# Norm, pick tables and mask of a fused four-layer kernel in PSUM banks, and two MLA steps in another order

## The reference, cut to what matters

```python
# 1. gMLP: layer norm of v (256 x 2048) ahead of the spatial product
u, v, g = jnp.split(rms_norm(h) @ w_in, 3, axis=-1)
v = layer_norm(v, ln_g, ln_b)                       # over 2048, one scale and one bias row
sv = jnp.einsum('gts,bcsgd->bctgd', wsm, v) + bs    # 16 groups, causal 128 x 128
y = u * sv * silu(g)
# 2. windowed attention ("b"): 16 heads of 64, keys of this and the block before, a sink per head
scores = jnp.where(mask, q @ k.T * 64 ** -0.5, -jnp.inf)
m = jnp.maximum(max(scores), sink)
p = exp(scores - m);  denom = sum(p) + exp(sink - m)
# 3. product-key experts, twice: 8 heads, 2 x 128 sub-keys, top 16 of each half
s1, i1 = top_k(s[:, :, 0], 16);  s2, i2 = top_k(s[:, :, 1], 16)
cand = s1[..., :, None] + s2[..., None, :]          # 16 x 16 sums of each head
top_s, pos = top_k(cand, 16)                        # pos // 16 picks from i1, pos % 16 from i2
# 4. MLA: c_q, c_kv, k_rope = split(x @ w_in); q = rms_norm(c_q) @ w_uq; kv = rms_norm(c_kv) @ w_ukv
```

## Time and profile before

| | us |
|---|---|
| median of 3 runs | 2416.28 |
| lowest, highest | 2414.76, 2420.68 |
| the profiled execution: its own time | 2416.68 |
| its span in the trace | 2414.9 |
| PE busy in the span | 2298.3 (95%) |
| PEld, DVE, ACT, POOL busy | 2100.4, 1470.9, 1167.3, 1175.9 |
| granted PE clock, mean | 0.986 of full |

### The profile page before, as it was taken

The page is one execution under the profiler, slowest core; times in us unless marked ns, Lnnn a source line. Parts: engine busy times, 40 slices in busy tenths (PEclk is TensorE's granted clock), DMA queues, the critical chain, the costliest instruction groups (busy, mean ns, idle before and its releaser), DMA issues. The chain is left out here.

```text
span 2414.9 us, 44964 instructions
## 1 busy us (share of the span) xinstructions
PE 2298.3 (95%) x15008; PEld 2100.4 (87%) x15008; DVE 1470.9 (61%) x3079; ACT 1167.3 (48%) x1775; POOL 1175.9 (49%) x491
## 2 busy tenths in 40 slices
PE   7999879999999999999999997799999999999998
PEld 5897868898999999998888887699999999888886
DVE  5533452342499766647777754419976664677777
ACT  5445534353444677753333334344457775433333
POOL 6967618666789766660000024369876666100000
PEclk9999999999999999999999999899999999999999
DMA  7544415545455444456556543244554444666653
GB/s 262 165 146 162 170 35 169 180 136 187 151 171 173 164 140 139 140 175 204 193 192 210 193 164 122 86 159 159 178 169 139 139 139 164 204 193 194 209 192 131
DMA packets 109594, 398.31 MB, mean 165 GB/s; under 512 B 12752, under 2 KB 13136, under 8 KB 108752
## 3 DMA queue, kind: packets, MB, share of 16 engines
q1 hardware_dynamic: 104688, 380.16, 47.3%
q10 hardware_dynamic: 4832, 17.17, 2.0%
HBM read 394.13 MB, written 3.15 MB: 165 GB/s over the span
## 5 line engine op out<-in xcount | busy, mean ns | idle before, releaser
L1963 POOL TENSOR_TENSOR w_lo<-ring,w_hi 128x1024 fp32r<-128x1024 f32 x474 | 1169.3, 2492 | 886.2 <-ACT w_hi L914 885.7
L914 ACT ACTIVATE w_hi<-ring 128x1024 fp32r<-128x1024 f32 x722 | 743.4, 1057 | 548.9 <-PE X L427 403.2
L425 PE MATMUL G<-hT_hi,w_hi 128*128 128x256 f32 x2880 | 826.2, 287 | 21.6 <-POOL w_lo L1963 17.6
L426 PE MATMUL G<-hT_lo,w_hi 128*128 128x256 f32 x2880 | 817.0, 284 | 0.0
L427 PE MATMUL G<-hT_hi,w_lo 128*128 128x256 f32 x2880 | 816.8, 284 | 0.0
L425 PEld LDWEIGHTS G<-hT_hi,w_hi 128*128 128x128 f32 x2880 | 554.3, 192 | 27.0 <-POOL w_lo L1963 21.7
L426 PEld LDWEIGHTS G<-hT_lo,w_hi 128*128 128x128 f32 x2880 | 554.6, 193 | 0.3 <-issue 0.2
L427 PEld LDWEIGHTS G<-hT_hi,w_lo 128*128 128x128 f32 x2880 | 554.1, 192 | 0.0
L425 PE MATMUL X<-w_hi,hT_hi 128*128 128x512 f32 x1024 | 398.4, 389 | 0.0
L426 PE MATMUL X<-w_lo,hT_hi 128*128 128x512 f32 x1024 | 398.4, 389 | 0.0
L427 PE MATMUL X<-w_hi,hT_lo 128*128 128x512 f32 x1024 | 398.3, 389 | 0.0
(11 more groups left out here) (283 smaller groups left out, 2332.5 us busy)
## 6 DMA issues: line engine op xcount, KB each, us to landing
ring<-slabs_in SPq DMA_DIRECT2D x722, 512.0 KB, 4.3
big<-rows_in ACTq DMA_DIRECT2D x10, 512.0 KB, 7.4
big<-rows_in ACTq DMA_DIRECT2D x3, 1024.0 KB, 7.5
big<-keys_in ACTq DMA_DIRECT2D x2, 1024.0 KB, 8.1
h_kept<-h ACTq DMA_DIRECT2D x2, 1024.0 KB, 10.7
h<-h_kept ACTq DMA_DIRECT2D x2, 1024.0 KB, 5.9
big<-ws_in ACTq DMA_DIRECT2D x1, 1024.0 KB, 13.6
out<-h SPq DMA_DIRECT2D x4, 256.0 KB, 2.3
```

The source lines that it names most:

```text
L425: nc.tensor.matmul(out, a_hi, b_hi, start=start, stop=False, skip_group_check=True)
L426: nc.tensor.matmul(out, a_hi, b_lo, start=False, stop=False, skip_group_check=True)
L914: nc.scalar.activation(w_hi[:, 2 * j + half, :], ring[j][:, half * 1024:(half + 1) * 1024], ACT.Copy).then_inc(hi_ready, 1)
L1963: Q.tensor_tensor(w_lo[:, 2 * j + half, :], ring[j][:, half * 1024:(half + 1) * 1024], w_hi[:, 2 * j + half, :], ALU.subtract).then_inc(sp ...
```

## The change

The two pairs of X banks are declared as two tensors of two banks each (`XX`), so that one instruction can work on 1024 elements. Then:

- The spatial norm works in halves of 1024: the first pass reads SBUF and writes PSUM, the second reads and writes PSUM, the third reads PSUM and writes SBUF; each of the last two has one SBUF operand, the scale or bias row. Twelve passes of 1024 take the place of six of 2048.
- The pick tables: the first half's tops and the cast of L1738 are copied to PSUM, the comparison and the product are written to a pair of banks in two halves of four heads, and the sum reads them there.
- Attention b: PE adds the mask into the bank (identity times mask, one product of 512 columns a unit) ahead of the scores; DVE takes the maximum from the bank and scales it when it is compared with the sink; ACT takes the exponentials from the bank and releases it. POOL makes two rounded copies, of the identity and of the mask, after the mask.
- MLA: `m_qn` goes ahead of `m_ck` and `m_krt`, on PE, ACT and in the bank order; DVE's rest of the k and v latents follows the rotation of q's part.
- At the last slab of `u0` and `u1` ACT rounds the next slab's weights before the Gelu of that slab, not after it.

```diff
-        X = [ctx.enter_context(nc.psum_tensor(f"X{i}", [P, 512], f32)) for i in range(4)]
+        XX = [ctx.enter_context(nc.psum_tensor(f"XX{i}", [P, 2, 512], f32)) for i in range(2)]
+        X = [XX[i // 2][:, i % 2, :] for i in range(4)]
...
-    ("m_tr", 4), ("m_ct", 2), ("m_qr", 2), ("m_ck", 1), ("m_krt", 1), ("m_qn", 4), ("m_kv", 8), ("m_qrt", 2),
+    ("m_tr", 4), ("m_ct", 2), ("m_qr", 2), ("m_qn", 4), ("m_ck", 1), ("m_krt", 1), ("m_kv", 8), ("m_qrt", 2),
...  # b_scores, on PE
+                nc.tensor.matmul(tile[:, :].rearrange("p (a k) -> p a k", k=keys), ident_r[:, :],
+                                 bc(B_mask_r[:, T - keys:], 1, len(heads)), start=True, stop=False, skip_group_check=True)
                 for a, hd in enumerate(heads):
                     last = nc.tensor.matmul(tile[:, a * keys:(a + 1) * keys], B_qT[:, hd // 2, queries],
-                                            kT[hd % 2][:, hd // 8, 0:keys], start=True, stop=True)
+                                            kT[hd % 2][:, hd // 8, 0:keys], start=False, stop=True, skip_group_check=True)
...  # MLA, on PE
-                if j == 0:
-                    keys_transposed()
+            keys_transposed()
             x_read(pe, "m_ck")
...  # the expert layer, on ACT (n == 63)
+                        split(SLAB0[f"u{l}"] + n + RING)
                     gelu_in_place(n % 4, n)
-                    split(SLAB0[f"u{l}"] + n + RING)
+                    if n < 63:
+                        split(SLAB0[f"u{l}"] + n + RING)
...  # MLA, on ACT
+            for i in range(4):
+                tile, free = x_tile(act, "m_qn", i)
+                nc.scalar.activation(flat(M_qn)[:, 512 * i:512 * (i + 1)], tile[:, :], ACT.Copy).then_inc(free, 1)
+                if i % 2:
+                    split(SLAB0["m_kv"] + i // 2)
             round_latents("m_ck", 0, (3, 4))
...  # attention, on DVE
-                        link(V.tensor_tensor(mx[:, m], mx[:, m], sink, ALU.max))
+                        link(V.scalar_tensor_tensor(mx[:, m], mx[:, m], scale, sink, ALU.mult, ALU.max))
...  # spatial norm, on DVE
             for b in range(NB):
-                last = V.tensor_scalar(A_v[:, b, :], A_v[:, b, :], mv[:, b, 0:1], rstd[:, b:b + 1], ALU.subtract, ALU.mult)
...
+                for part, bank in zip(parts, banks):
+                    last = V.tensor_scalar(bank, A_v[:, b, part], mv[:, b, 0:1], rstd[:, b:b + 1], ALU.subtract, ALU.mult)
+                link(last)
+                for part, bank in zip(parts, banks):
+                    last = V.tensor_tensor(bank, bank, A_lng[:, part], ALU.mult)
+                link(last)
+                for part, bank in zip(parts, banks):
+                    last = V.tensor_tensor(A_v[:, b, part], bank, A_lnb[:, part], ALU.add)
...  # attention b, on DVE: the mask pass goes
-                V.scalar_tensor_tensor(s, tile[:, :].rearrange("p (a k) -> p a k", a=n), DH ** -0.5,
-                                       bc(B_mask[:, T - keys:], 1, n), ALU.mult, ALU.add).then_inc(free, 1)
...  # pick tables, on DVE
+                    first = X[2][:, 0:PK_H * TOPK].rearrange("p (n k) -> p n k", k=TOPK)
+                    link(V.tensor_copy(first, tops[:, :, 0, :]))
+                    link(V.tensor_tensor(K_cand.rearrange("p n (a b) -> p n a b", a=16), bc(first, 3, 16),
                                          bc(tops[:, :, 1, :], 2, 16), ALU.add))
...
-                        link(V.tensor_copy(K_af, K_au))
-                        link(V.tensor_tensor(K_eq, bc(K_af, 3, 16), bc(bc(iota[:, 0:16], 1, 16), 1, PK_H), ALU.is_equal))
-                        link(V.tensor_tensor(K_eq, K_eq, bc(index[:, :, c, :], 2, 16), ALU.mult))
-                        link(V.tensor_reduce(picks[:, b, c, :].rearrange("p (n k) -> p n k", k=TOPK), K_eq, AX.X, ALU.add))
+                        link(V.tensor_copy(place, K_au))
+                        chosen = picks[:, b, c, :].rearrange("p (n k) -> p n k", k=TOPK)
+                        equal = XX[0][:, :, :].rearrange("p a (n k j) -> p (a n) k j", n=2, k=TOPK)
+                        for heads in (slice(0, 4), slice(4, 8)):
+                            link(V.tensor_tensor(equal, bc(place[:, heads, :], 3, 16), bc(bc(iota[:, 0:16], 1, 16), 1, 4),
+                                                 ALU.is_equal))
+                            link(V.tensor_tensor(equal, equal, bc(index[:, heads, c, :], 2, 16), ALU.mult))
+                            link(V.tensor_reduce(chosen[:, heads, :], equal, AX.X, ALU.add))
...  # MLA, on DVE
-            rest_latents("m_ck", 0, (3, 4))
             for i in range(2):
...
+            rest_latents("m_ck", 0, (3, 4))
...  # the mask, on POOL
+            Q.tensor_copy(ident_r[:, :], ident[:, :])
+            Q.tensor_copy(B_mask_r, B_mask).then_inc(sem("b_mask_ready"), 1)
```

More of the change, by code:

```diff
@@ L1033, in take_rows, with attention @@
                                              ACT.Copy).then_inc(free, 1)
-            def attention(name, sinks, from_psum=None, round_to=None):
+            def attention(name, sinks, scale, round_to=None):
                 for kind, k in attention_order(name):
@@ L1044, in attention @@
                             nc.scalar.activation(esink[:, row:row + n], esink[:, row:row + n], ACT.Exp)
-                        if from_psum:
-                            tile, free = x_tile(act, stage, 0)
+                        tile, free = x_tile(act, stage, 0)
                         for u in range(n):
-                            src = tile[:, u * T:(u + 1) * T] if from_psum else s[:, u, :]
-                            last = nc.scalar.activation(s[:, u, :], src, ACT.Exp, bias=negm[:, row + u:row + u + 1],
-                                                        scale=from_psum or 1.0,
+                            keys = s.shape[2]
+                            last = nc.scalar.activation(s[:, u, :], tile[:, u * keys:(u + 1) * keys], ACT.Exp,
+                                                        bias=negm[:, row + u:row + u + 1], scale=scale,
                                                         accum_out=rsum[:, row + u:row + u + 1])
-                        last.then_inc(free if from_psum else sem(f"exp_{name}"), 1)
+                        last.then_inc(free, 1)
                     elif kind == "t":
@@ L1135, in _ @@
             take_T("b_qtr", B_qT)
-            attention("b", True)
+            attention("b", True, DH ** -0.5)
             seam("b_out", "fin", "r_v", lambda: round_block("r_tr", hT_hi, 0))
@@ L1259, in _ @@
             nc.scalar.activation(M_krTo[64:128, :], tile[64:128, 0:T], ACT.Copy).then_inc(free, 1)
[L1260 to L1264, removed]
             for i in range(MLA_H):
@@ L1425, in rotate_bank, with attention @@
                 last.then_inc(done, 1)
-            def attention(name, sinks, prepare, take_values):
+            def attention(name, sinks, scale, prepare, take_values):
                 def maximum(k):
@@ L1520, in _ @@
             stats("vn", [A_v[:, b, :] for b in range(NB)], True)
-            for b in range(NB):
-                last = V.tensor_scalar(A_v[:, b, :], A_v[:, b, :], mv[:, b, 0:1], rstd[:, b:b + 1], ALU.subtract, ALU.mult)
-            link(last)
             dve.wait_ge(sem("rows_loaded"), 16 * 6)
             for b in range(NB):
[L1526 to L1529, removed]
+                parts = [slice(q * 1024, (q + 1) * 1024) for q in range(2)]
+                banks = [XX[q][:, :, :].rearrange("p a n -> p (a n)") for q in range(2)]
+                for part, bank in zip(parts, banks):
[6 more added lines that the diff above has]
+                    last = V.tensor_tensor(A_v[:, b, part], bank, A_lnb[:, part], ALU.add)
+                if b == 0:
+                    link(last)
             last.then_inc(sem("vn_ready"), 1)
@@ L1602, in _, with b_unit @@
             take_T("b_qtr", B_qT)
[L1603 to L1609, removed]
-                V.scalar_tensor_tensor(s, tile[:, :].rearrange("p (a k) -> p a k", a=n), DH ** -0.5,
-                                       bc(B_mask[:, T - keys:], 1, n), ALU.mult, ALU.add).then_inc(free, 1)
-                x_read(dve, f"b_s{k}")
-                return s
+            def b_unit(k):
+                n = units["b"][k][0].shape[1]
+                tile, _ = x_tile(dve, f"b_s{k}", 0)
+                return tile[:, :].rearrange("p (a k) -> p a k", a=n)
             def b_gated(k):
@@ L1624, in _ @@
             g_read(dve, "b_g")
-            attention("b", True, b_masked, b_gated)
+            attention("b", True, DH ** -0.5, b_unit, b_gated)
             def final_norm(tiles, b):
@@ L1930, in m_unit @@
                 return tile[:, :].rearrange("p (b k) -> p b k", b=NB)
-            attention("m", False, m_unit, m_rest)
+            attention("m", False, float(P + ROPE) ** -0.5, m_unit, m_rest)
             first = add_first("m_out", ALPHA)
@@ L1983, in _ @@
```

(6 more changed lines are left out.)

16 lines of the change are left out of this document (10 added, 6 removed).

## The result

| | before | changed |
|---|---|---|
| median, beside each other on one chip (6 runs each) | 2417.75 | 2405.5 (2401.9 to 2407.63) |
| ratio, 95% interval | | 0.9949 [0.9936, 0.9962] |
| profiled execution, its span, clock | 2416.7, 2414.9, 0.986 | 2405.4, 2403.7, 0.979 |
| PE, DVE, POOL busy | 2298.3, 1470.9, 1175.9 | 2311.7, 1402.9, 1137.9 |

What follows compares the result with a forecast made beforehand. PE, busy 95% in a fixed order, was taken as the bound, with about 117 us idle. Terms -5.1 + 0.8 - 6.0 - 15.8 - 3.0 = -29.1 us took 2416.7 to 2387.6, stated as 2388; range 2380 to 2401.

Steps and rivals of the forecast that it cites:

- the MLA term: MLA reorder: -4.7 us from earlier k and v work, about 1.7 back for two stalls at lower clock: -3.0.
- Rival 3: MLA gives nothing: the tail is as long or the clock stays low; 2391 to 2392 us, 0.15 shared with the bank rival.
- Pick tables: Expert layers' tables: PSUM operands free POOL from wide DVE passes, 7.9 us in each of two layers: -15.8 us.
- rival 2: Norm and tables: new DVE passes still take turns with POOL, half the gain stays; 2398 us, chance 0.10.
- rival 4: Norm and tables: PSUM operands take turns with POOL just the same; about 2445 us, chance 0.04.
- Spatial norm: Norm beside a_u: twelve passes of 1.22 us through PSUM leave POOL undisturbed, -5.1 us.
- the unknown of this part: Norm's first pass, SBUF to PSUM, not in the trace: between 1.22 and 3.6 us, taken as 1.22.
- POOL's copies: Two rounded copies at the mask, ahead of a_u, make PE wait longer: +0.8 us, bounds 0.5 and 1.3.
- Attention b: Mask pass moved off DVE, which bounds each unit: period from 2.71 to about 2.0 us, -6.0 us.
- rival 1: Attention b: the score bank becomes the bound, period no shorter than 2.71 us; 2394 to 2397, 0.15 shared with MLA's rival.
- Gelu after the split: Seam at slab 63: PE doesn't wait there and the later Gelu is covered, 0 us; without cover 2 x 2.

Runs made afterwards that it cites:

- experiment 3: Changed kernel with twelve unread 128x512 products filling PE's idle time between the transposes and the wait for the latents' rest, ahead of m_kv: 2390.55 us, 0.9881.
- experiment 5: Changed kernel with twenty 128x512 products, overwritten after, between the stall of 3.1 us and the first m_kv product: 2396.11 us, 0.9916.
- experiment 12: Changed kernel with sixty 128x128 products, overwritten after, between the stall of 3.1 us and the first m_kv product: 2418.5 us, 1.0001.
- experiment 8: Kernel before with the spatial norm's part of the change alone: 2410.98 us, 0.9975.
- experiment 10: Kernel before with attention b's part alone (mask through PE, maximum and exponentials from the bank, POOL's two copies): 2415.79 us, 0.9991.
- experiment 4: Changed kernel without its MLA part, plus a wait ahead of the first m_kv product for ACT's split of k and v's second slab: 2408.44 us, 0.995.

## Why the prediction was wrong, step by step

**The failed step is the MLA term**, and in it one clause: "two stalls of 2.5 and 4 us should cost about 1.7 at the lower clock". Two stalls came, of 2.59 and 3.14 us, and the arrival was right too (-3.5 where -4.7 and 1.7 of slow products make -3.0). The price of the second was not a few us of slow products but a whole stage: 16.7 us by the ledger, with the filler of experiment 3 (149.7) and without it (166.4). I had taken the price from the earlier trace rows, where q's products get the clock back 6.1 us after a stall of the same kind. The change moved a stall in front of other products, and experiments 5 and 12 show that these are what counts. Why the clock comes back under some shapes and not under others stays open. Rival 3 named the mechanism ("or the clock stays low") but let it only cancel the gain; its time of 2391 to 2392 was too low by 14.

**Pick tables: right.** -15.8 forecast, -16.9 by the medians, 7.8 in each layer by the ledger. ACT's takes of slabs 1 and 23 in `u0`, against the earlier trace rows, then groups of DVE and POOL from 640 to 790 us, against the earlier trace rows:

```profile
641.62 0.60 ACT L1182 ACTIVATE big<-G 128x512 f32 x1 [2.00 <-PE G L430]
...
768.49 0.60 ACT L1182 ACTIVATE big<-G 128x512 f32 x1 [3.27 <-PE G L430]
```

```profile
L1751 DVE TENSOR_TENSOR XX<-XX,iota 128x1024 f32<-128x1024 f32 x8 | 9.9, 1232 | 0.3
L1753 DVE TENSOR_TENSOR XX<-XX,big 128x1024 f32<-128x1024 f32 x8 | 9.9, 1232 | 0.3
L1754 DVE TENSOR_REDUCE picksT<-XX 128x64 f32<-128x1024 f32 x8 | 9.8, 1224 | 0.3
...
L1976 POOL TENSOR_TENSOR w_lo<-ring,w_hi 128x1024 fp32r<-128x1024 f32 x54 | 128.8, 2415 | 35.2 <-ACT w_hi L919 35.2
```

126.87 us for 22 slabs, 5.77 each; passes of 1.23 us where 1.22 was estimated; POOL at 2.415 us, undisturbed beside passes that run all the time. That also refutes rivals 2 and 4. By the rule on the shared ports that the prediction cites (the Trainium skill, SBUF — State Buffer, section "SBUF: two separate sides"), DVE takes them for an operation with two SBUF inputs or in a two-port mode. None of the new wide passes has two SBUF inputs, and the trace agrees with 2.4 us a half of POOL beside them.

**Spatial norm: right.** -5.1 forecast, -6.0 [-8.7, -3.6] measured alone, and in that trace the takes of `a_u` are 40.32 us from first to last instead of 45.42. POOL's halves in that stage, in the kernel before (74 to 120 us) and in the changed one (76 to 118 us):

```profile
L1963 POOL TENSOR_TENSOR w_lo<-ring,w_hi 128x1024 fp32r<-128x1024 f32 x15 | 44.6, 3001 | 3.8 <-ACT w_hi L914 3.7
...
L1976 POOL TENSOR_TENSOR w_lo<-ring,w_hi 128x1024 fp32r<-128x1024 f32 x15 | 35.7, 2403 | 9.1 <-ACT w_hi L919 9.1
```

The first pass, the unknown of this part, and the two others in the changed kernel:

```profile
85.32 2.59 DVE L1530 TENSOR_SCALAR XX<-big,mv,rstd 128x1024 f32<-128x1024 f32 x2
87.95 2.37 DVE L1533 TENSOR_TENSOR XX<-XX,big 128x1024 f32<-128x1024 f32 x2
90.35 2.36 DVE L1536 TENSOR_TENSOR big<-XX,big 128x1024 f32<-128x1024 f32 x2
```

**POOL's copies: too cheap.** Forecast +0.8 us, bounds 0.5 to 1.3. The waiting itself was right; POOL and PE, against the earlier trace rows:

```profile
64.50 0.29 POOL L1999 CAST ident_r<-ident 128x128 fp32r<-128x128 f32 x1
64.73 0.40 POOL L2000 CAST B_mask_r<-big 128x256 fp32r<-128x256 f32 x1
...
67.79 0.39 PE L428 MATMUL G<-hT_hi,w_hi 128*128 128x256 f32 x1 [2.18 <-POOL w_lo L1976]
68.60 0.32 PE L428 MATMUL G<-hT_hi,w_hi 128*128 128x256 f32 x1
68.72 0.41 PE L429 MATMUL G<-hT_lo,w_hi 128*128 128x256 f32 x1
```

PE's stall went from 1.50 to 2.18 us, and at 68.7 the products became slower (0.21 apart, granted clock 0.50) until 72.1: 1.5 us more. From the last take of `a_v` to the first of `a_u` it is 9.68 us with the copies and 7.52 without (experiment 8): +2.2. In experiment 10, with the same 2.18 us of stall, the clock held and it was 8.20: +0.7. It is the MLA error in small: a stall was lengthened, and only its length was priced. Of the nine profiled executions with this stall of 2.2 us the clock fell behind it in six and held in three; behind the 1.5 us without the copies it held in all four.

**Attention b: right in the mechanism, uneven in the size.** The unit takes 1.98 us as forecast (2.0), PE idles 0.23 in it (0.2 to 0.5), and the bank is never the bound: in the changed kernel's list of waits PE has none for ACT's exponentials ahead of L643 or L646 (rival 1 falls).

```profile
310.52 0.66 PE L589 MATMUL XX<-ident,big 128*128 128x128 f32 x4 [0.23 <-DVE big L1455]
310.93 0.47 PE L643 MATMUL XX<-B_mask_r,ident_r 128*128 128x512 f32 x1
311.24 1.03 PE L646 MATMUL XX<-big 128*128 128x256 f32 x4
312.50 0.66 PE L589 MATMUL XX<-ident,big 128*128 128x128 f32 x4 [0.23 <-DVE big L1455]
```

By the ledger slabs 42 to 47 take 97.5 to 97.7 us in the four profiled executions with the old attention, 91.6 to 91.8 in seven with the new one, and 93.4 to 95.1 in the four others with it. So the gain is 5.8 us mostly, and 2.5 to 4.2 in the rest, depending on how long the clock stays at 0.50 in this stage: 17.1 us in all seven, 20.5 in the one of 93.4, 23.9 in the three of 94.7 to 95.1. This part alone measured -2.2 [-4.4, 0] where -5.2 was forecast: in its profiled execution the stage gained 2.8 us and the copies cost 0.7.

**Gelu after the split: right.** 0; slabs 120 to 214 take 567.25 us in both. It was not run alone.

## What to carry to other kernels

A stall of TensorE is priced by the products that follow it, not by its length alone: look in the trace which products regain the granted clock after a stall and which only hold it, and let no stall of 2 to 3 us end in front of the latter. When steps are reordered, follow the longest tail that was hidden before (here copy, split, rounding, rest) to the product that now waits for it, and put independent wide products beside it. And read the share of PE busy with care: the changed kernel's rose from 95% to 96% for that very reason.

## What the runs showed of the hardware

- At a granted clock of 0.50, sixty products of 128x128 and then those of `m_kv` left it at 0.50 for about 45 us with PE busy nearly all the time (experiment 12); fewer than twenty of 128x512, or 3.4 to 6.1 us of 128x256 products, brought it back to 1.00 (experiment 5; 1447.73 us in the changed kernel and 1465.56 in the kernel before). Which property of the products decides was not measured beyond these shapes.
- The same stall brings the clock down in some executions and not in others: 2.2 us ahead of `a_u` in six of nine profiled ones, 2.24 us ahead of the first `m_qr` product in seven of fifteen, and, by the times alone, 2.62 us in five of six runs of experiment 4. The Trainium skill (TensorE: Matmul & The Clock Gate, section "HAM oscillation — how this bites in real kernels") tells of bursts of products that start slow after each wait. The traces agree with that, and add that the slow stretch can outlast the wait more than tenfold (41 us after 3.14).
- A first pass from SBUF into PSUM took 1.30 us for 1024 elements, the in-place passes in PSUM 1.18 to 1.23, with POOL at its own 2.4 us beside them.
